# Four blocks of an operand moved to four other addresses modulo 512 in the FFNs of a fused two-block network

## The reference

```python
for l in range(2):
    h = h + 0.5 * swiglu(rmsnorm_2(h, ffn_pre_norm[l]), wg, wu, wd)     # FFN 1 and FFN 3
    u = rmsnorm_2(h, mix_norm[l])
    h = h + (pool_mixer(u, ...) if l == 0 else mla_attention(u, ...))
    h = h + 0.5 * swiglu(rmsnorm_2(h, ffn_post_norm[l]), wg, wu, wd)    # FFN 2 and FFN 4
return rmsnorm_2(h, final_norm)

def swiglu(u, wg, wu, wd):
    return (silu(u @ wg) * (u @ wu)) @ wd      # u 512x1024, wg and wu 1024x2816, wd 2816x1024
```

## The kernel before

| tensors | bytes past the weights, modulo 512 |
|---|---|
| whi, wlo, sxhi, sxlo, chi, clo, xghi, xglo, ahi, alo, oThi, oTlo | 0 |
| Xhi0, Xlo0, Xhi1, Xlo1, Xhi2, Xlo2, Xhi3, Xlo3 | 288 |
| bands, from column 16 of band w = 0, 1, 2, 3 | 64, 192, 320, 448 |

## Time and profile before

### The profile page before, as it was taken

The page is one execution under the profiler, slowest core; times in us unless marked ns, Lnnn a source line. Parts: engine busy times, 40 slices in busy tenths (PEclk is TensorE's granted clock), DMA queues, the critical chain, the costliest instruction groups (busy, mean ns, idle before and its releaser), DMA issues.

```text
span 2346.3 us, 33505 instructions
## 1 busy us (share of the span) xinstructions
PE 2321.3 (99%) x13510; PEld 2020.8 (86%) x13510; DVE 1661.6 (71%) x1666; ACT 1008.6 (43%) x1277; POOL 842.6 (36%) x441
## 2 busy tenths in 40 slices
PE   8999999999999999999999999999999999999998
PEld 7889788888789999989899879899967778799997
DVE  5687587772489687669696769696777743696874
ACT  5324443442355344554354454353543342453443
POOL 1320222121046456348256328355311001474551
PEclk9999999999999999999999999999999999999999
DMA  5221232323323332323332332333221122233322
GB/s 162 86 72 55 72 108 89 107 85 99 103 72 107 110 108 86 105 79 105 107 122 83 91 117 91 108 113 103 91 68 40 45 72 90 90 99 109 117 86 85
DMA packets 220050, 219.29 MB, mean 93 GB/s; under 512 B 10897, under 2 KB 217360, under 8 KB 219920
## 3 DMA queue, kind: packets, MB, share of 16 engines
q1 hardware_dynamic: 218992, 215.27, 28.9%
q10 hardware_dynamic: 928, 2.17, 0.4%
HBM read 213.22 MB, written 2.10 MB: 92 GB/s over the span
## 4 chain that ended last, share of the span: by engine, by line
PE 85%; POOL 6%; DVE 3%; DMA 2%; ACT 2%; issue 1%; SPq 0%; DVEq 0%; ACTq 0%; POOLq 0%
PE bank L1356 16%; PE bank L1358 15%; PE bank L1357 15%; PE bank L1350 10%; PE bank L1352 10%; PE bank L1351 10%; POOL sums L668 2%; POOL raw L669 2%; PE bank L1994 2%; PE bank L2041 2%; PE bank L1997 1%; POOL sums L671 1%; PE bank L1485 1%; POOL sums L673 1%; DMA raw<-in_ffn_pre_wu_dram 1%
## 5 line engine op out<-in xcount | busy, mean ns | idle before, releaser
L1350 PE MATMUL bank<-Xhi,wlo 128*128 128x256 f32 (+1 forms) x1283 | 374.1, 292 | 4.2 <-DVE Xlo L2342 2.8
L1351 PE MATMUL bank<-Xlo,whi 128*128 128x256 f32 (+1 forms) x1283 | 373.1, 291 | 0.0
L1352 PE MATMUL bank<-Xhi,whi 128*128 128x256 f32 (+1 forms) x1283 | 373.0, 291 | 0.0
L668 POOL TENSOR_TENSOR sums<-raw 128x512 f32<-128x512 f32 x72 | 147.4, 2047 | 429.2 <-DMA raw<-in_ffn_post_wg_dram 162.9
L1031 ACT ACTIVATE whi<-raw 128x2048 fp32r<-128x2048 f32 x72 | 138.3, 1920 | 371.5 <-PE bank L1358 223.9
L1350 PE MATMUL bank<-Xhi,sxlo 128*128 128x256 f32 (+1 forms) x960 | 280.8, 292 | 0.3
L1351 PE MATMUL bank<-Xlo,sxhi 128*128 128x256 f32 (+1 forms) x960 | 278.9, 291 | 0.0
L1352 PE MATMUL bank<-Xhi,sxhi 128*128 128x256 f32 (+1 forms) x960 | 278.9, 291 | 0.0
L1350 PEld LDWEIGHTS bank<-Xhi,wlo 128*128 128x128 f32 x1283 | 241.8, 188 | 11.7 <-issue 4.5
L1351 PEld LDWEIGHTS bank<-Xlo,whi 128*128 128x128 f32 x1283 | 241.7, 188 | 6.4 <-issue 0.5
L1352 PEld LDWEIGHTS bank<-Xhi,whi 128*128 128x128 f32 x1283 | 241.8, 188 | 5.8
(11 more groups left out here) (378 smaller groups left out, 5567.6 us busy)
## 6 DMA issues: line engine op xcount, KB each, us to landing
raw<-in_ffn_w_up_dram SPq DMA_DIRECT2D x22, 1024.0 KB, 5.1
raw<-in_ffn_pre_wg_dram SPq DMA_DIRECT2D x22, 1024.0 KB, 5.3
raw<-in_ffn_pre_wu_dram SPq DMA_DIRECT2D x22, 1024.0 KB, 5.4
raw<-in_ffn_post_wg_dram SPq DMA_DIRECT2D x22, 1024.0 KB, 5.3
raw<-in_ffn_post_wu_dram SPq DMA_DIRECT2D x22, 1024.0 KB, 5.3
raw<-in_ffn_pre_wd_dram SPq DMA_DIRECT2D x24, 768.0 KB, 4.8
raw<-in_ffn_post_wd_dram SPq DMA_DIRECT2D x24, 768.0 KB, 4.9
raw<-in_w_in_dram SPq DMA_DIRECT2D x13, 1024.0 KB, 5.0
```

What stands on the lines that cost most here:

```text
L668: nc.gpsimd.tensor_tensor(s1, a21, a22, ALU.add).then_inc(adds_done[h], 1)
L1350: nc.tensor.matmul(bank, wl, x, start=first, stop=False, skip_group_check=True)
L1351: nc.tensor.matmul(bank, w, xl, start=False, stop=False, skip_group_check=True)
L1352: return nc.tensor.matmul(bank, w, x, start=False, stop=last, skip_group_check=True)
```

## The change

The gap of 72 floats (288 bytes) ahead of slots 2 and 3 goes. Instead a gap stands ahead of each of the four blocks: 16 floats (64 bytes) before Xhi2, Xlo2 and Xhi3, and 32 floats (128 bytes) before Xlo3. The blocks' starts become 200384, 207616, 214848 and 222144, which are 64, 128, 192 and 320 bytes past the weights modulo 512; Xlo3 ends at 229312. Slots 0 and 1, all other tensors, all instructions and all waits stay.

```diff
@@ -231,9 +231,10 @@
         spans = sb("spans", [P, 5 * SPAN], F32, pl)
         inv = sb("inv", [P, 4 * 16], F32, pl)
         pl.close()
-        sb("x_gap", [P, 72], F32, f2)
         for j in range(2, 4):
+            sb(f"xhi_gap{j}", [P, 16], F32, f2)
             Xhi[j] = sb(f"Xhi{j}", [P, 7 * HT], F32R, f2)
+            sb(f"xlo_gap{j}", [P, (16, 32)[j - 2]], F32, f2)
             Xlo[j] = sb(f"Xlo{j}", [P, 7 * HT], F32R, f2)
         f2.close()
```

## The result

| | before | after |
|---|---|---|
| median of 20 runs each | 2346.04 us | 2350.23 us |
| ratio of the runs, 95% interval | | 1.0017 (1.0011 to 1.0023) |
| span of the profiled execution | 2346.3 us | 2351.6 us |

What follows compares the result with a forecast made beforehand. PE was taken to bound the kernel; +10.1 us for narrow and -2.5 us for wide matmuls sum to +7.6 us on 2345.3, forecasting 2352.9 us (chance 0.38, own range 2349 to 2356), overall range 2325 to 2360.

Steps and rivals of the forecast that it cites:

- What bounds the kernel, and what to count: Whole kernel: PE holds a matmul for 2321.3 of 2346.3 us; the distance between matmul starts is what to count.
- The count of what is touched: Matmuls reading slots 2 and 3 only: 3024 of 6048 narrow ones and 384 wide ones; slots 0 and 1 stay.
- The price of the new classes: x blocks at 64, 128, 192, 320 past the weights: all priced like class 0, 120.0 ns narrow, 226.7 wide.
- The term of +10.1 us for the narrow matmuls: Slots 2 and 3: 3024 narrow (256-column) matmuls each 3.33 ns dearer, +10.1 us.
- The term of -2.5 us for the wide ones: Slots 2 and 3: 384 wide (512-column) matmuls each 6.5 ns cheaper, -2.5 us.
- steps of 3.33 ns: Narrow matmuls: the difference from class 288's 116.67 ns to class 0's 120.0 ns, charged per matmul.
- All of it reaches the end: Stretches where PE has no slack: what the matmuls lose or gain goes to the end one for one.
- Whether the distance to the weights matters: Matmul at 752.22 without a concurrent weight load lasted 0.28 us like others: weak evidence against a clash with the load.
- No change: Rival for the whole kernel: no change, or effects that cancel; chance 0.25.
- Faster: Rival for the whole kernel: the change gains time, 2316 to 2341 us; chance 0.29.
- The jump as a cost: Rival, slots 2 and 3: class jumps cost another +10.1 us on top of class 0's price, 2363 us; chance 0.08.
- `bands`: Pooling's plain fp32 matmuls at 64, 192, 320, 448: groups 1.16 us apart, so multiples of 64 were taken as alike.

Runs made afterwards that it cites:

- The dearest, 96: All x blocks 96 bytes past the weights, against the kernel before: 18.9 us slower.
- experiment 1: All eight x blocks at class 0 (0 bytes past the weights, modulo 512), against the kernel before: 2360.02 us against 2346.81, ratio 1.0055.
- experiment 3: Every tensor 32 bytes higher, distances to the weights kept, against the kernel before: 2347.01 us against 2346.81, ratio 1.0003.
- experiment 12: Against the changed kernel: slots 0 and 1 at 320, Xhi2 at 64, Xlo2 and Xhi3 at 192, Xlo3 at 320; 2346.18 us against 2345.91 before.
- experiment 4: Slots 2 and 3 all at class 64, slots 0 and 1 at 288, against the kernel before: 2347.26 us against 2346.81, ratio 1.0004.

## Why the prediction was right, and where it was not

*What bounds the kernel, and what to count.* Right. In the stretches of the earlier trace rows PE is idle for 0.08 us at most, at a granted clock of 1.00, so that only the distance between starts can change their length, and in all thirteen other kernels the time follows it, to within 2.5 us and mostly a little less than it. The dearest, 96, has 6048 x 3.30 = +20.0 us in its narrow matmuls and +0.1 in the wide ones, and is 18.9 us slower; all at 0 has 6048 x 3.29 - 759 x 6.47 = +15.0, and is 13.2 slower.

*The count of what is touched.* Wrong. The sum let only the 3024 narrow matmuls of slots 2 and 3 pay. Half of the new cost lies in the other two slots: the slots 0 and 1 have 1512 x 1.04 and 1512 x 1.12 = 3.3 us together, slot 2 has 0.9 and slot 3 2.3. The prediction named this as what would show the count wrong.

*The price of the new classes.* The step that put all four with class 0 because they are multiples of 64 was wrong. Alone, 64, 192 and 320 cost 117.7 ns narrow and only 128 costs 120.0. The term of +10.1 us for the narrow matmuls measured 6048 x 1.07 = +6.5, of which the own prices make 6048 x 0.69 = 4.2 and the mixture 2.3. The term of -2.5 us for the wide ones measured 759 x 0.98 = -0.7, since at 128 and 192 a wide matmul costs 232.8 and 233.3 ns and at 64 and 320 some 229, not 226.7. The sum counted in steps of 3.33 ns, which is the earlier trace rows less. No run shows the prices to go by such a step: 117.7 ns stand 1.0 above 116.7, and the three distances at 128 are 117.5, 120.0 and 122.5 ns, 2.5 apart. What was right is class 0's price itself, which experiment 1 gave back to 0.2 ns.

*All of it reaches the end.* Nearly. +6.5 and -0.7 make +5.7, the runs show +4.0. The twelve stretches, each from its first start to the first start of the down projection behind it, add up to 707.8 us before and 712.3 after, +4.5, while the matmuls alone are 705.8 and 712.3: before held 2.0 us of waits in them, in 16 distances over 140 ns, and after holds one of 202 ns. The loads' group in the page before and in the page after:

```profile
L1350 PEld LDWEIGHTS bank<-Xhi,sxlo 128*128 128x128 f32 x960 | 180.4, 188 | 6.0 <-ACT kept L1070 1.1
```

```profile
L1351 PEld LDWEIGHTS bank<-Xhi,sxlo 128*128 128x128 f32 x960 | 180.3, 188 | 4.6 <-issue 0.5
```

The wait for ACT to keep a partial sum (`keep`, L1070), of which the earlier trace rows show one, is gone: slower matmuls reach that point when ACT is already done. In the first stretch PE starts the last matmul ahead of that point at 753.38 us, 1.16 later than in the earlier trace rows, and ACT begins the copy at 753.06, only 0.90 later than before. It is also why the PE of the first window has 59.00 us where the earlier trace rows had 58.92. The 759 wide ones with their waits take 180.3 us before and 179.9 after, -0.4. With +4.5 for the stretches the sum is +4.1, well inside the interval of 2.6 to 5.4; the spans differ by 0.8 us more, which arises in the first 193 us, where nothing reads an x block.

*Whether the distance to the weights matters.* Read wrongly. The one matmul beside which no load ran lasted 0.28 us like all others, and the text took this, weakly, for a sign that the load has no part in it. Experiment 3 shows that the distance from the standing operand counts and the address does not. Whether the load is what gets in the way stays open: in experiment 1 the loads lengthen with the matmuls, from 188 to 192 ns, at 96 the matmuls cost as much and the loads take 187 to 190. The end of a matmul is modelled; the row could not carry that.

*The rivals.* No change, chance 0.25: the price varies by 3.3 ns with the class, and this mixture came to a third of that, 1.07 ns. Faster, chance 0.29, from 2316 to 2341 us: no run shows a time in that range nor the terms that would give one, and the lowest median of the moved kernels is the 2346.18 us of experiment 12. Narrow against class 0 and wide against 288, the new classes save in both widths at 64 and 320 (117.7 ns for 120.0, 229 for 233), at 192 only in the narrow ones and at 128 hardly in either (120.0 and 232.8 ns), and no class went under 116.7 when alone. The jump as a cost: present here with 2.3 us where a step of 10.1 was set, and experiment 12 shows a mixture that gains. `bands`, alike at 64, 192, 320 and 448, did not carry over to fp32r: they showed no difference between 64 and 192 where wide fp32r matmuls have 229.1 and 233.3 ns. Six of these plain fp32 matmuls, of 144 or 128 columns, start in 0.71 us in the kernel before (993.95 to 994.66 us), 0.85 ns a column where a narrow fp32r one has 116.7/256 = 0.46; the rows at that lower rate did not show what the fp32r ones pay.

The direction was right and the range held the time; the size was about twice what came, from one term mis-sized in price, one in reach, and 2 us of waits that gave way. That the time even fell within 2349 to 2356, the forecast's own range, is partly luck: with the right prices the sum's own count gives +4.2 in the narrow ones, and 2.3 us for the mixture, which it left out, and 2.0 us of waits, which it did not know of, nearly cancel.

## What to carry to other kernels

Where PE is the bound and its clock is full, read the distance from start to start by operand before anything else; two operands that are streamed in the same shape can differ by 3% (116.7 and 120.0 ns, 226.9 and 234.2). The place of the moving operand against the standing one, in SBUF, is a thing to tune, and it is cheap to try: put all blocks of a kind at one distance, take the trace, and read the price of that distance from the first and the last of many starts, over whole chains. Try the mixture that you mean to ship as a whole, since blocks that did not move can change their cost.

## What the runs showed of the hardware that was not expected

- The distance between moving and standing fp32r operands sets what a matmul costs in a full stream, and it repeated after 256 bytes on the two pairs tried (0 and 256, 64 and 320): 116.7 to 120.0 ns for 256 columns and 226.9 to 234.2 for 512 over the classes tried. The two widths have different best places: 288 is best for narrow and 6.5 ns from the best for wide.
- Moving both together by 32 bytes changed neither width's cost (116.74 and 233.32 ns).
- With x at 0 or 256 the weight loads take 192 ns, at 288, 64 and 320 they take 187 to 189. That would point to the load and the stream getting in each other's way, but at 192 one of three loads takes 192 ns with a cheap narrow matmul, and at 96, the dearest, they take 187 to 190. No run took the load away; the mechanism is open.
- With all blocks of one class the distances inside a chain can still be uneven, 117.5, 120.0 and 122.5 ns at 128 and slots of 119.1 to 120.9 at 96, with 120.0 as the mean in both. Why is open.
- In a mixture, slots that did not move went from 116.7 up to 117.8 (the change) and 119.0 (experiment 4), and single steps went down to 114.2 ns (experiment 12). Classes 32, 352, 384 and above were not run on their own.
